# Two-layer hybrid trunk with a routed expert layer: the heads of the expert rounds split from the loop, a second feature buffer, and a PSUM bank of its own for the last down product

## The chip, the cores and the metric

The kernel runs on one core of a Trainium2 chip. The metric is the time of one execution on the device in microseconds (us); lower is better. The engines are TensorE (PE in the profile, its weight loads PEld), VectorE (DVE), ScalarE (ACT), GpSimd (POOL) and SyncE (SP). They run side by side and wait for each other through semaphores only.

## The reference, cut to what matters

Two layers run over 256 context tokens and 256 latent tokens of width 1024, all in float32. Each has a mixer (retention, state-space scan, neighbourhood attention), which the change leaves alone, and then a mixture of 16 experts of which every token takes two:

```python
def moe_ffn(h, router_w, router_b, w_gate, w_up, w_down):
    t = h.reshape(-1, shp[-1])
    aff = jax.nn.sigmoid((t @ router_w).astype(jnp.float32))
    ...  # best group of four experts, then its top 2: idx; gates = affinities over their sum
    # each chosen expert e:  (silu(t @ w_gate[e]) * (t @ w_up[e])) @ w_down[e]
    # weighted by the gate, summed over the two, times a gate row of the layer, added to the stream
```

Layer 0 routes 512 tokens (T = 4 tiles of 128), layer 1 only the 256 latent ones (T = 2). The expert weights of a layer are 16 x 3 x 2 MB, and all of them are read.

## The kernel before, in words

`route` (DVE) finds the chosen experts and gates. `assign` (DVE, L1980 to L2011) counts the tokens of each expert, ranks the experts by load, gives each a capacity (128, 96 or 64 slots by rank), works out how many rounds R are needed (an overfull expert needs a second one; here one runs), writes the order of the experts to `order_i`, from which SP reads which weights to load, and at its end (L2008 to L2011) works out `place`, each token's slot in its expert. Experts 0 and 1 always have the first two ranks, since `route` sets their keys so.

Then every engine loads the number of rounds into a register (`load_rounds`) and enters a loop over rounds. DVE opens it with the memset L2164, whose semaphore `round_dve` the other engines wait for. An expert position q goes through these steps. The positions are grouped in units of one gather: a big or middle expert is a unit of its own, two small ones share one.

- `slots_of(u)` (DVE, three operations, L2032, L2037, L2040): which token owns each slot of unit u, as a one-hot sum; `who(u)` on PE (L1153) turns it into a column, `who(u)` on DVE (L2047) makes the indices `slot_i`, and POOL gathers the rows of the tokens (`gather`, L2314).
- `turn_x(u)` (PE, L1162) transposes the rows and ACT copies them (L1512) to one half of `XT`.
- `wide(q, 0)` and `wide(q, 1)` (PE, L1185, L1188, L1191) are the gate and up products, ACT's `silu` (L1519) and DVE's `product` (L2055) make the feature `hp`, `turn_h(q)` (PE, L1201) transposes it, ACT's `turned_h` (L1528) copies it to `hT`, `down(q)` (PE, L1217, L1221) is the down product to bank 3 (with bank 4 where it is wide), and DVE's `result` (L2069, for the joined ones L2066) takes it to `Yb`.
- ACT stores `Yb` to DRAM (L1536, L1540). After the last expert, POOL gathers each token's two rows back (L2340), ACT scales one (L1568), and DVE adds, gates and adds to `h` (L2136 to L2141 in layer 1, L2156 to L2161 in layer 0).

The order on PE is written by hand: in position q come wide(q, 0), turn_h(q-1), wide(q, 1), then turn_x and who of later units, then down(q-1). SP's queue issues the loads of the weights in order over 8 buffers (L682), each when the product that read the buffer before is done; the first load past the six early ones also waits for both first gathers.

In layer 1 the last two positions are "joined": they are not stored and gathered back, but a product with a slot matrix (`join`, L1248) puts them onto the tokens, and DVE adds that to `h` (`add_joined`, L2148). There the last down product already has bank 4 for itself, there are two `hT` buffers, and turn_h(15) stands ahead of down(14). In layer 0 there is one `hT`, and turn_h(15) comes after down(14):

```python
                        if plan.joined and q == NE - 1:
                            turn_h(r, q)
                        if q > 0:
                            down(r, q - 1)
                    ...
                    if not plan.joined:
                        turn_h(r, NE - 1)
                    down(r, NE - 1)
```

At the end of layer 1, DVE's queue has `add_gathered(0)` ahead of `result(14)`, and `add_gathered(1)` ahead of `result(15)`; each is three operations over 128x1024.

## Time and profile before

| | us |
|---|---|
| median of 3 runs (lowest, highest) | 1318.07 (1317.95, 1320.23) |
| the profiled execution | 1317.74 |
| its span, first to last instruction | 1315.9 |
| TensorE busy, share of the span | 1161.7, 88% |
| mean granted TensorE clock | 0.947 |
| DMA | 318.87 MB, mean 242 GB/s |

The span is the part of the execution that the profile shows; 1.84 us of the profiled execution lie outside it. All times in rows count from the span's start. "Idle before" stands in brackets with what ended it; a granted clock of 1.00 is 2.4 GHz and 0.50 is 1.2 GHz.

### The profile page before, as it was taken

How to read it: one execution, taken by the hardware profiler on the slowest of the kernel's cores; microseconds unless marked ns; L12 is line 12 of the kernel's file. 1: busy time of each engine (PE TensorE's matmuls, PEld its weight loads, DVE VectorE, ACT ScalarE, POOL GpSimd, SP SyncE). 2: the span in 40 equal slices, each digit the busy share in tenths (PEclk: the TensorE clock that was granted, in tenths of full speed). 3: DMA queues.
4: the chain of work that ended last, by engine and by line, in shares of the span. 5: the costliest groups of instructions: out<-in, count | busy, mean ns of one | idle time of the engine just before them, and what ended most of it. 6: DMA issues, size and time to landing. Idle time of an engine off the chain costs nothing.

```text
span 1315.9 us, 17739 instructions
## 1 busy us (share of the span) xinstructions
PE 1161.7 (88%) x7360; PEld 653.9 (50%) x7360; DVE 403.9 (31%) x759; ACT 219.7 (17%) x417; POOL 136.1 (10%) x118
## 2 busy tenths in 40 slices
PE   4899998999999389999999189998999579999875
PEld 1444444767644245654564055554865355645442
DVE  0131123794322741212111423034832531111004
ACT  2120221112220411110010222131121210111101
POOL 0002011550000010000000200211400010000001
PEclk9799999989999779999999689999999879999998
DMA  9222114652370478999997541137517469999995
GB/s 380 108 109 78 65 64 172 245 191 80 134 299 9 184 281 339 399 425 422 427 424 268 165 169 64 64 128 261 218 65 320 160 268 374 411 426 426 428 427 216
DMA packets 34481, 318.87 MB, mean 242 GB/s; under 512 B 6497, under 2 KB 7649, under 8 KB 16737
## 3 DMA queue, kind: packets, MB, share of 16 engines
q1 hardware_dynamic: 22432, 292.03, 55.3%
q10 hardware_dynamic: 7072, 13.11, 2.8%
q0 software_dynamic: 4896, 12.59, 2.7%
q8 instruction: 59, 0.97, 0.3%
q14 instruction: 22, 0.17, 0.0%
HBM read 308.79 MB, written 14.16 MB: 245 GB/s over the span
## 4 chain that ended last, share of the span: by engine, by line
PE 77%; DMA 11%; DVE 7%; ACT 2%; issue 2%; SPq 0%; POOL 0%; DVEq 0%; ACTq 0%; POOLq 0%
PE ps L843 14%; PE ps L1185 12%; PE ps L1087 6%; PE ps L830 6%; PE ps L1217 6%; PE ps L1188 4%; DMA ring<-in_w_mod 3%; DMA arena<-in_w_down 3%; PE ps L776 3%; PE ps L1191 2%; PE ps L1000 2%; DMA arena<-in_w_gate 2%; PE ps L1226 2%; PE ps L1162 2%; PE ps L1016 2%
## 5 line engine op out<-in xcount | busy, mean ns | idle before, releaser
L843 PE MATMUL ps<-ring,featT 128*128 128x512 f32 (+1 forms) x480 | 186.9, 550 | 0.0
L843 PEld LDWEIGHTS ps<-ring,featT 128*128 128x128 f32 x480 | 90.7, 190 | 92.3 <-issue 89.9
L1185 PE MATMUL ps<-arena 128*64 128x256 f32 x896 | 104.5, 387 | 5.9 <-ACT arena L1512 2.4
L2055 DVE TENSOR_TENSOR arena<-arena,ps 128x256 f32<-128x256 f32 (+2 forms) x32 | 15.6, 488 | 254.5 <-PE ps L1185 132.1
L1185 PEld LDWEIGHTS ps<-arena 128*64 128x64 f32 x896 | 64.7, 139 | 43.4 <-issue 15.8
L830 PE MATMUL ps<-featT,ring 128*128 128x512 f32 (+1 forms) x192 | 82.5, 588 | 2.3 <-ACT featT L1337 2.3
L1087 PE MATMUL ps<-ring,featT 128*128 128x512 f32 x192 | 82.7, 592 | 0.0
L2069 DVE COPY arena<-ps 128x512 f32<-128x512 f32 (+2 forms) x30 | 25.0, 834 | 142.2 <-PE ps L1217 65.5
L2314 POOL DMA_INDIRECT arena<-ffn_rows,slot_i x22 | 24.1, 1094 | 412.0 <-DVE slot_i L2047 412.0
L1519 ACT ACTIVATE arena<-ps 128x256 f32<-128x256 f32 (+2 forms) x32 | 14.0, 437 | 308.6 <-PE ps L1185 144.4
L1188 PE MATMUL ps<-arena 128*128 128x512 f32 x128 | 59.5, 622 | 2.3 <-ACT arena L1512 2.3
L830 PEld LDWEIGHTS ps<-featT,ring 128*128 128x128 f32 x192 | 36.8, 194 | 45.8 <-issue 42.6
L1087 PEld LDWEIGHTS ps<-ring,featT 128*128 128x128 f32 x192 | 36.5, 190 | 45.9 <-issue 45.9
L806 PE MATMUL ps<-const,tokA 128*128 128x128 f32 x112 | 20.3, 360 | 37.7 <-DVE tokA L1639 35.9
L1217 PE MATMUL ps<-arena 128*64 128x512 f32 x192 | 47.6, 605 | 3.8 <-DMA arena<-in_w_down 3.8
L776 PE MATMUL ps<-ring,silT 128*32 128x256 f32 (+1 forms) x656 | 48.0, 413 | 0.0
L1185 PE MATMUL ps<-ring,arena 128*64 128x256 f32 x384 | 44.1, 382 | 3.7 <-DMA ring<-in_w_gate 2.6
L1512 ACT ACTIVATE arena<-ps 128x1024 f32<-128x1024 f32 x22 | 22.5, 1023 | 124.6 <-PE ps L1162 124.6
L1188 PEld LDWEIGHTS ps<-arena 128*128 128x128 f32 x128 | 24.9, 199 | 33.6 <-issue 32.1
L2233 POOL TENSOR_TENSOR stat<-stat,pw 128x5 f32<-128x5 f32 (+2 forms) x14 | 14.6, 1044 | 258.2 <-DVE stat L1634 213.2
L806 PEld LDWEIGHTS ps<-const,tokA 128*128 128x128 f32 x112 | 18.5, 191 | 42.3 <-DVE tokA L1639 38.4
L1672 DVE COPY arena<-ps 128x512 f32<-128x512 f32 (+1 forms) x16 | 10.0, 625 | 93.1 <-PE ps L843 93.1
(314 smaller groups left out, 1611.2 us busy)
## 6 DMA issues: line engine op xcount, KB each, us to landing
ring<-in_w_mod SPq DMA_DIRECT2D x21, 2048.0 KB, 8.2
arena<-in_w_up SPq DMA_DIRECT2D x20, 2048.0 KB, 16.7
arena<-in_w_gate SPq DMA_DIRECT2D x16, 2048.0 KB, 16.8
ring<-in_w_down SPq DMA_DIRECT2D x12, 2048.0 KB, 13.3
arena<-in_w_down SPq DMA_DIRECT2D x12, 2048.0 KB, 17.7
ring<-in_w_in SPq DMA_DIRECT2D x10, 2048.0 KB, 7.9
ring<-in_w_gate SPq DMA_DIRECT2D x8, 2048.0 KB, 18.9
ring<-in_w_out SPq DMA_DIRECT2D x4, 2048.0 KB, 8.3
```

The lines of the kernel that those rows point to most:

```text
L776: i = mm(mod_row(l, u)[g:g + 32, :], silT[:, k, :], piece(q)[:, k, c:c + mod_width(l)], start=k < 4, stop=k >= 4)
L806: i = tr(ps[:, 1 + k % 4, P * t:P * t + P], tokA[:, t, P * k:P * k + P], ident)
L830: o = mm(bank[:, lo:TOK], W[:, k, c:c + P], featT[:, k, lo:TOK], start=k == 0, stop=k == KD - 1)
L843: o = mm(bank[:, lo:hi], featT[:, k, P * i:P * i + P], W[:, k, lo:hi], start=k == 0, stop=k == KD - 1)
L1000: i = mm(ps[:, 6 + t // 2, 256 * (t % 2):256 * (t % 2) + 256], featT[:, k, P * t:P * t + P], nvw[:, k, :], start=k == 0, stop=k == KD - 1)
L1016: i = mm(ps[:, n % 2, 0:keys], naT[s, hd // 2, P * t:P * t + P], naT[s, 2 + hd // 2, 0:keys], start=True, stop=not lat)
L1087: i = mm(ps[:, 4 + n % 2, :], featT[:, k, P * t:P * t + P], piece(p)[:, k, :], start=k == 0, stop=k == KD - 1)
L1162: o = tr(ps[:, 5 + k // 4, P * (k % 4):P * (k % 4) + P], gathered[u % 2][:, P * k:P * k + P], ident)
L1185: o = mm(ps[64 * half:64 * half + 64, m, 0:256], X_[:, k, at:at + SMALL_CAP], W[:, k, 256 * half:256 * half + 256], start=k == 0, stop=k = ...
L1188: o = mm(ps[:, m, :], X_[:, k, :], W[:, k, :], start=k == 0, stop=k == KD - 1)
L1191: o = mm(ps[32 * g:32 * g + 32, m, 256:384], X_[:, k, SMALL_CAP:SMALL_CAP + 32], W[:, k, P * g:P * g + P], start=k == 0, stop=k == KD - 1)
L1217: o = mm(ps[64 * out_half:64 * out_half + 64, to, :], H_[:, b, 64 * half:64 * half + 64], W[:, k, 512 * out_half:512 * out_half + 512], st ...
```

## The change

It has four parts, besides the counts of the semaphores that follow from them.

1. **Heads.** `place` is worked out at the start of `assign`, and slots_of, who and gather of units 0 and 1 leave the loop: slots_of(0) follows `place`, the others are put between the steps that rank the experts. PE and POOL do their parts ahead of `load_rounds`. Inside the loop each round now prepares the first two units of the round after it, also in the last round, where no token is left for them: per layer two more slots_of, who and gather. For that the subtraction from `place` (L2197) moves from the round's end to the position that opens the last unit but one.
2. **Layer 0's last product.** `hT` has two buffers in layer 0 too, turn_h(15) comes ahead of down(14), and down(15) goes to bank 4 and waits for result(13) only. ACT's turned_h(15) goes ahead of store(14).
3. **Layer 1's results.** Every `result` multiplies by the layer's gate row, in two operations over 64 partitions (six for a middle expert). ACT's scaling and one DVE operation for each tile drop out: `add_gathered` becomes two operations straight onto `h`.
4. **Layer 1's end.** DVE's order is result(14), add_gathered(0), result(15), add_gathered(1), add_joined. The rows gathered back go to other buffers.

```diff
 PE
@@ experts @@
+                for u in range(2):
+                    who(round_of(l, rounds_run[-1], 0), u)
+                first, R = load_rounds(pe, l)
+                rounds_run.append(R)
                 with pe.Fori(0, R) as n_round:
                     pe.wait_ge(S("round_dve"), r.all + (l + 1))
-                    who(r, 0)
-                    who(r, 1)
                     turn_x(r, 0)
...
-                        if plan.opens(q) and u + 2 < len(units):
+                        if plan.opens(q):
+                            if plan.joined and u + 1 == len(units):
+                                pe.wait_ge(S("slots_act"), n_round + 1)
                             who(r, u + 2)
-                        if plan.joined and q == NE - 1:
+                        if q == NE - 1:
                             turn_h(r, q)
                         if q > 0:
                             down(r, q - 1)
-                    if not plan.joined:
-                        turn_h(r, NE - 1)
                     down(r, NE - 1)
@@ down @@
-                    last = q == NE - 1 and q in plan.joined
+                    last = q == NE - 1
                     if q > 0:
                         pe.wait_ge(S("y_dve"), r.all * NE + (q - 1 if last else q))
                     to = 4 if last else 3
-                    H_ = hT_joined[q % 2] if plan.joined else hT
+                    H_ = hT_two[q % 2]
 ACT
@@ experts @@
+                        if q == NE - 1:
+                            turned_h(r, q)
                         if q > 0 and q - 1 not in plan.joined:
                             store(r, q - 1)
...
-                    turned_h(r, NE - 1)
                     if not plan.joined:
                         store(r, NE - 1)
-                    for i in range(T):
+                    for i in range(0 if plan.joined else T):
 DVE
@@ assign @@
+                link(V.tensor_scalar(pl, heads(ps[:, 3, 0:NE * T], T), 4096.0, None, ALU.add))
+                link(V.tensor_tensor(pl[:, 1:T, :], pl[:, 1:T, :], sums[:, 0:T - 1, :], ALU.add))
+                link(V.tensor_tensor(pl, pl, ch, ALU.mult))
+                link(V.tensor_scalar(pl, pl, -4096.0, None, ALU.add))
+                r = round_of(l, rounds_run[-1], 0)
+                slots_of(l, r, 0)
                 link(V.scalar_tensor_tensor(key[:, 2:NE], count[:, 2:NE], float(NE), iota[:, 2:NE], ALU.mult, ALU.subtract))
                 link(V.tensor_tensor(perm[:, :, :], repeat(key, NE), spread(key, NE), ALU.is_gt))
+                who(l, r, 0)
+                slots_of(l, r, 1)
                 link(V.tensor_reduce(rank, perm[:, :, :], AX.X, ALU.add))
                 ...
+                who(l, r, 1)
                 link(V.reciprocal(load_of, capE))
                 ...
-                (the four lines of place)
@@ result, layer 1 @@
-                    if q in plan.joined:
+                    if plan.joined:
+                        bank = 4 if q == NE - 1 else 3
                         for half in range(2):
                             s = slice(64 * half, 64 * half + 64)
-                            o = V.tensor_tensor(Yb[s, q % 2, 0:512], ps[s, 3 + q % 2, :], grow[s, 1, 512 * half:512 * half + 512], ALU.mult)
+                            o = V.tensor_tensor(Yb[s, q % 2, 0:512], ps[s, bank, :], grow[s, 1, 512 * half:512 * half + 512], ALU.mult)
+                        for g in range(4 if plan.middle(q) else 0):
+                            s = slice(32 * g, 32 * g + 32)
+                            o = V.tensor_tensor(Yb[s, q % 2, 512:768], ps[s, 4, 0:256], grow[s, 1, 256 * g:256 * g + 256], ALU.mult)
@@ add_gathered @@
+                    for n in range(2):
+                        ...
+                        V.scalar_tensor_tensor(h[:, t, :], back_joined[q - 1 + n], gate2[:, 1 - n, t:t + 1], h[:, t, :], ALU.mult, ALU.add
+                                               ).then_inc(S(("both_dve", "gated_dve")[n]), 1)
@@ experts @@
-                    for u in range(2):
-                        slots_of(r, u)
-                        who(r, u)
                     rows_of_round(r)
                     for q in range(NE):
                         u = plan.unit_of(q)
-                        if plan.opens(q) and u + 2 < len(units):
-                            slots_of(r, u + 2)
+                        if plan.opens(q) and u + 2 == len(units):
+                            V.tensor_tensor(pl, pl, repeat(capE, T), ALU.subtract).then_inc(S("row_steps"), 1)
+                            ...
+                        if plan.opens(q):
+                            slots_of(l, r, u + 2)
                         product(r, q)
-                        if plan.opens(q) and u + 2 < len(units):
-                            who(r, u + 2)
-                        if plan.joined and q == NE - 1:
-                            add_gathered(0)
+                        if plan.opens(q):
+                            who(l, r, u + 2)
                         if q > 0:
                             result(r, q - 1)
                     if plan.joined:
-                        add_gathered(1)
+                        add_gathered(0)
                     result(r, NE - 1)
                     if plan.joined:
+                        add_gathered(1)
                         for i in range(T):
                             add_joined(i)
...
+                    for c in range(2):
+                        dve.wait_ge(S(f"gathered{c}"), r.gathers + (len(units) // 2 * 16 + 16))
 POOL
@@ experts @@
+                for u in range(2):
+                    gather(round_of(l, of_layer_0, 0), u)
+                first, R = load_rounds(pool, l)
                 with pool.Fori(0, R) as n_round:
                     pool.wait_ge(S("round_dve"), r.all + (l + 1))
-                    for u in range(len(units)):
+                    for u in range(2, len(units) + 2):
                         gather(r, u)
```

## Rows read from the trace of the kernel before

**Rows 1.** The page: POOL's DMA queue (packets, MB, share); the chain that ended last.

```profile
q0 software_dynamic: 4896, 12.59, 2.7%
...
PE 77%; DMA 11%; DVE 7%; ACT 2%; issue 2%; SPq 0%; POOL 0%; DVEq 0%; ACTq 0%; POOLq 0%
```

**Rows 2.** Stretches of layer 1: busy us (instructions) by engine, clock, DMA share, GB/s.

```profile
1060.00:1070.00 10.00, 8.04 (x60) 5.25 (x64) 5.33 (x23) 2.31 (x2) 0.93 (x1) 0.60 0.57 200
...
1116.00:1118.00 2.00, 2.00 (x19) 1.09 (x17) 0.00 (x0) 0.00 (x0) 0.00 (x0) 1.00 0.78 270
...
1260.00:1270.00 10.00, 7.72 (x58) 4.48 (x56) 0.69 (x1) 0.75 (x2) 0.00 (x0) 1.00 1.01 429
```

**Rows 3.** Timeline of layer 0's head: start, us, engine, line, operation, idle before.

```profile
448.40 0.17 DVE L1986 SCALAR_TENSOR_TENSOR arena<-arena,const 128x14 f32<-128x14 f32 x1
...
453.62 0.22 DVE L2008 TENSOR_SCALAR arena<-ps 128x64 f32<-128x64 f32 x1
...
455.56 0.06 DVE L2164 MEMSET arena<- 128x1 f32 x1 [0.98 <-DVE arena L2011]
...
455.80 0.69 DVE L2032 TENSOR_TENSOR arena<-const,arena 128x512 f32<-128x512 f32 x1 [0.19 <-issue]
...
458.33 0.59 PE L1153 MATMUL ps<-const,arena 128*128 128x1 f32 x2 [11.28 <-DVE arena L2040]
...
464.74 1.97 PE L1162 MATMUL ps<-const,arena 128*128 128x128 f32 x8 [2.61 <-DMA arena<-ffn_rows,slot_i]
```

**Rows 4.** Timeline of layer 1's head.

```profile
1054.20 0.06 DVE L2164 MEMSET arena<- 128x1 f32 x1 [1.34 <-issue]
...
1054.36 0.43 DVE L2032 TENSOR_TENSOR arena<-const,arena 128x256 f32<-128x256 f32 x1
...
1055.76 0.59 PE L1153 MATMUL ps<-const,arena 128*128 128x1 f32 x2 [9.20 <-DVE arena L2040]
...
1060.76 1.97 PE L1162 MATMUL ps<-const,arena 128*128 128x128 f32 x8 [2.33 <-DMA arena<-ffn_rows,slot_i]
```

**Rows 5.** Timeline of layer 0's end.

```profile
721.27 0.42 DVE L2055 TENSOR_TENSOR arena<-arena,ps 128x256 f32<-128x256 f32 x1 [6.66 <-PE ps L1185]
...
724.53 0.44 PE L1201 MATMUL ps<-const,arena 128*128 128x128 f32 x2
...
727.10 3.65 PE L1217 MATMUL ps<-ring,arena 128*64 128x512 f32 x16 [2.13 <-ACT arena L1528]
...
757.10 0.23 DVE L2197 TENSOR_TENSOR arena<-arena 128x64 f32<-128x64 f32 x1 [0.16 <-DVE h L2161]
```

**Rows 6.** Timeline of the SP queue in layer 1: weight loads.

```profile
1064.22 0.35 SPq L682 DMA_DIRECT2D featT<-in_w_gate  x1
...
1117.04 0.33 SPq L682 DMA_DIRECT2D arena<-in_w_up  x1
```

**Rows 7.** Chain in order of time, layer 1: start, us, what.

```profile
1181.80 3.43 PE ps L1217 x16
...
1193.80 3.58 PE ps L1217 x16
```

**Rows 8.** Timeline of layer 1's end.

```profile
1278.04 0.69 DVE L2069 COPY arena<-ps 128x512 f32<-128x512 f32 x1 [4.84 <-PE ps L1217]
...
1293.83 0.94 POOL L2340 DMA_INDIRECT h<-expert_rows,arena  x1 [0.31 <-issue]
...
1294.70 3.65 PE L1217 MATMUL ps<-ring,arena 128*64 128x512 f32 x16 [1.25 <-DMA ring<-in_w_down]
...
1297.28 1.28 DVE L2136 SCALAR_TENSOR_TENSOR arena<-h,arena 128x1024 f32<-128x1024 f32 x1 [8.62 <-DMA h<-expert_rows,arena]
...
1301.00 1.38 DVE L2066 TENSOR_TENSOR arena<-ps,arena 64x512 f32<-64x512 f32 x2
...
1306.25 1.39 DVE L2066 TENSOR_TENSOR arena<-ps,arena 64x512 f32<-64x512 f32 x2
...
1311.61 1.22 DVE L2148 TENSOR_TENSOR h<-h,ps 128x1024 f32<-128x1024 f32 x1 [0.48 <-PE ps L1248]
```

More of the change, by code:

```diff
@@ L564, in trunk @@
         PLANS = [Plan(*TIERS[l], ORDERS[l], (NE - 2, NE - 1) if l == DEPTH - 1 else ()) for l in range(DEPTH)]
+        assert all(p.small(NE - 1) for p in PLANS)
         for q in PLANS[DEPTH - 1].joined:
@@ L1968, in route, with slots_of, who @@
                 link(V.tensor_tensor(ga, ga, spread(rsum[:, t0:NT], NE), ALU.mult))
+            rounds_run = [0]
+            def slots_of(l, r, u):
+                T, t0 = len(tiles(l)), tiles(l)[0]
+                plan = PLANS[l]
+                units = plan.units()
+                if u >= 2 or l > 0:
+                    dve.wait_ge(S("who_pe"), r.heads + (u - 1))
+                if u >= 1 or l > 0:
+                    dve.wait_ge(S("onehot_dve"), r.heads + u)
+                qs = units[u % len(units)]
+                v = plan.ranks[qs[0]]
+                n, each = len(qs), P // len(qs)
+                src = placeR if 2 <= u < len(units) else place
+                hot = onehot[:, 0:T, :]
+                V.tensor_tensor(hot.rearrange("p t (a s) -> p t a s", a=n),
+                                const[:, C_IOTA:C_IOTA + each].unsqueeze(1).unsqueeze(1).to_broadcast([P, T, n, each]),
+                                src[:, t0:NT, v:v + n].unsqueeze(3).to_broadcast([P, T, n, each]), ALU.is_equal
+                                ).then_inc(S("hot_steps"), 1)
+                dve.wait_ge(S("hot_steps"), 2 * r.heads + (2 * u + 1))
+                V.tensor_tensor(hot, hot, spread(const[:, C_TOK:C_TOK + T], P), ALU.mult
+                                ).then_inc(S("hot_steps"), 1)
+                dve.wait_ge(S("hot_steps"), 2 * r.heads + (2 * u + 2))
+                V.tensor_reduce(owner[:, u % 2, :], hot.rearrange("p t s -> p s t"), AX.X, ALU.add
+                                ).then_inc(S("onehot_dve"), 1)
+            def who(l, r, u):
+                dve.wait_ge(S("who_pe"), r.heads + (u + 1))
+                if u >= 2:
+                    dve.wait_ge(S(f"gathered{u % 2}"), r.gathers + (u // 2) * 16)
+                V.tensor_scalar(slot_i[:, u % 2:u % 2 + 1], ps[:, 7, 0:1], NO_TOKEN, None, ALU.add).then_inc(S("who_dve"), 1)
             def assign(l):
@@ L2308, in gather @@
                 def gather(r, u):
-                    pool.wait_ge(S("who_dve"), r.units + (u + 1))
+                    pool.wait_ge(S("who_dve"), r.heads + (u + 1))
                     if u >= 2:
@@ L2326, in experts @@
                     if plan.joined:
[L2327 removed]
+                        pool.wait_ge(S("up_pe"), r.all * NE + (NE - 2))
                     else:
```

97 lines of the change are left out of this document (31 added, 66 removed).

## The prediction

> **What bounds the kernel now.** I read the page first: TensorE has 77% of the chain that ended last, DMA 11%, VectorE 7% [rows 1]. That is a mean over stages, so I then read the stretches of the two expert stages, and in each looked for what ends last.
>
> In layer 0 TensorE never waits for weights: it runs without a gap from the first product to the last, and the stage is as long as TensorE's work. Time can be won there only ahead of the first product, where TensorE stands idle through a chain of small VectorE operations (it sat 11.28 us before who(0), and 2.61 us more for the gather [rows 3]), and behind the last ones.
>
> Layer 1 begins so too: in 1116 to 1118 the DMA share is 0.78, since the load at 1117.04 had to wait for TensorE [rows 2, 6]. From there on it does not fall again; in 1260 to 1270 it is 1.01 at 429 GB/s and TensorE is busy for 7.72 of 10 us [rows 2]. So the second half is bound by the weight stream. But that stream's last gap is closed by a product of TensorE, so an earlier TensorE moves the whole stream. Behind it stands a tail of VectorE work: down(15) ends at 1294.70 + 3.65 = 1298.35, the last addition at 1312.83 [rows 8].
>
> **Heads.** Nothing of the VectorE chain is dropped ahead of the first product; its order changes. Today the memset that opens the round stands at 455.56, and behind it come slots_of(0), who(0), the gather and turn_x(0) at 464.74 [rows 3]. Afterwards two slots_of and two who stand ahead of the memset. A slots_of takes 458.33 - 455.80 = 2.53 us in layer 0 and 1055.76 - 1054.36 = 1.40 in layer 1 [rows 3, 4]; who on VectorE I take at 0.1, below the 0.22 of another small operation there [rows 3]. TensorE's part of who is covered by the ranking steps that stand between. Memset: 455.56 + 2 x 2.53 + 2 x 0.1 = 460.8; turn_x(0) some 0.15 behind it, 461.0.
>
> Is the gather there by then? slots_of(0) starts at 448.40 plus the four operations of `place`, at most 455.56 - 453.62 = 1.94 together with the register loads. The one-hot is ready at 452.9, and from one-hot to turn_x went 464.74 - 458.33 = 6.41 us [rows 3]: 459.3, 1.7 us before it is needed. So the round's opening releases turn_x(0), no longer the gather. Layer 0 gains 464.74 - 461.0 = **3.7 us**. In layer 1 the memset comes at 1054.20 + 2.8 + 0.2 = 1057.2, turn_x at 1057.35 instead of 1060.76: **3.4 us**; one-hot to turn_x took only 5.00 us there [rows 4], so the gather is early again. Bounds: 2 us in each if every new wait costs a few tenths; 5.4 if the gather alone set it (459.3).
>
> In layer 1 the first of the later weight loads, now at 1064.22 behind both gathers [rows 6], can start up to 5 us earlier. I count nothing for it beyond the 3.4: the loads behind it wait for TensorE, up to the one at 1117.04.
>
> **Extra units.** Each layer gets two more who on TensorE. Cold, the pair of passes took 0.59 [rows 3]; warm and in the stream I take 0.15 each, **+0.3 us** in layer 0 (bounds 0 and 1.2) and nothing in layer 1, where TensorE waits for weights by then. VectorE's slots_of, 2.53 us at most, and the moved subtraction lie beside the gate and up products. From one down product to the next went 1193.80 - 1181.80 = 12.0 us, of which the down product itself is 3.4, so VectorE has over 8 us between them [rows 7]. The four empty gathers stand on POOL's queue ahead of the gathers back, which wait for the stores anyway, so they hold up nothing there. They do put packets into the DMA queues. POOL's queue had 4896 packets for 34 indirect DMAs, 144 each; its 12.59 MB are 3072 rows of 4 KB, so 1824 packets carried no row [rows 1]. Its share, 2.7% of the span, is 35.5 us; 12.59 MB at 429 GB/s are 29.3 [rows 1, 2]; 6.2 us are left for the 1824, 0.5 for a gather of 144. Only layer 1's two lie in a bound stream: **+1.0 us** (bounds: nothing, and 2.4 if each moved 128 rows of 4 KB).
>
> A page gives another price for them: the Trainium skill, "DMA: Bandwidth & Descriptors", section "Measured (HBM→SBUF, 128 partitions, SWDGE, issued from GpSimd)", names a floor of about 10.5 ns per packet. As an estimate from that page, 144 packets would take 1.5 us and two such gathers 3.0, which would bring the sum 2.0 us higher than the rows do. What the trace shows, packets that cost about a third of that on average, is what I take.
>
> **Layer 0's last product.** Today hp(15) is ready at 721.27 + 0.42 = 721.69, but turn_h(15) waits behind down(14) until 724.53, then for ACT's copy, so that down(15) starts at 727.10 [rows 5]. Afterwards TensorE idles for hp from 721.2, does turn_h to 722.25 (0.44), then down(14) in the 3.35 us it took (721.2 to 724.53) to 725.6, and down(15) directly behind: its `hT` is ready under down(14), its bank is its own. Gain 727.10 - 725.6 = **1.5 us**. result(14) comes 1.1 us later, but the last store, which the gathers back wait for, hangs on down(15). Bounds 1.0 and 2.1.
>
> L2197 stood on the chain at the layer's boundary with 0.23 us; two waits long since met take its place: **0.2 us**.
>
> **Layer 1's results.** Each small result becomes two operations of 64 partitions, 1.38 us for the pair against 0.69 for the copy; a middle one gets six, which I put at 2.9 [rows 8]. This lies in the 8 us between down products [rows 7]; if that cover were gone, it would be the rival below. One place is open: result(13) releases the store that the gathers back wait for, so these come 0.7 us later.
>
> **Layer 1's end.** Today `add_gathered(0)` started when the second gather landed, 1297.28, and result(15) had to wait for both add_gathered, to 1306.25, 8 us after down(15) had ended [rows 8]. Afterwards (stream unshifted): the second gather at 1297.9, two operations of 1.28 with the first already begun, to 1299.2; result(15) to 1300.65; add_gathered(1) to 1303.25 (its last gather was issued at 1293.83, and landing like the second takes it to about 1300.5); join beside it, done at the latest 1311.61 - 1307.64 = 3.97 us after result(15), at 1304.6; the last add_joined, 1.22, to 1305.85. Against 1312.83 that is **7.0 us**. Bounds: 5, if late gathers or the join end last; 8, if result(15) starts as soon as down(15) ends.
>
> **Sum.** 3.7 + 1.5 + 0.2 - 0.3 = 5.1 in layer 0; 3.4 - 1.0 + 7.0 = 9.4 in layer 1; 14.5 together. The profiled execution took 1317.74, so 1303.2; the median of the runs is 0.33 higher: **1303.5 us**.
>
> **Rivals.**
> (a) The stream of layer 1 does not follow: if DMA were the bound from its first load on, only that load's time would count and TensorE's earlier start would be lost, 1303.5 + 3.4 = 1306.9. For it speaks the share of 1.01 at the end; against it the gap at 1116 to 1118 [rows 2].
> (b) The reordering of layer 1's end brings only its lower bound, since the gathers back, issued under full DMA load, come later than today: 1305.5. For it, 8.62 us of VectorE's waiting for just that gather [rows 8]; against it, that they ran after the stores at the same distance from the stream's end.
> (c) More than forecast: the heads reach the gather's time (1.7 more in layer 0 and as much in layer 1) and the empty gathers cost nothing: 1299.1. Against it stands the order of the chain, which no one shortened.
> (d) Layer 0's new order does not do what it is to do, since turn_h(15)'s stall ahead of down(14) eats the gain: 1305.0. Layer 1 runs this order already, but there weights end last, so its trace does not settle it.
> (e) Slower: the doubled results get onto TensorE's path in layer 1. If down(q+1) waited for result(q) at every position, it would be 12 x 1.38 + 4 x 2.9 = 28 us, 1331. It decides once VectorE's work between two down products (product, slots_of, two or six result operations, at most about 6 us) passes the 8 us [rows 7]. I see nothing that takes it there.
>
> TensorE's clock adds spread to all: in 1060 to 1070 it was granted 0.60 on the mean, so four fifths of that stretch ran at 1.2 GHz after the idle head [rows 2]. If the rise comes 2 us earlier or later against the work, that is 1 us each way in each layer.
>
> **How the numbers follow.** Forecast within 1301 to 1305.3: 0.57. (a) 0.13, (b) 0.09, (d) 0.06, (c) 0.10, (e) 0.02, no measurable change for reasons I don't see 0.03. The range reaches from (c)'s edge to a little beyond (a): 1299.5 to 1307.5. A change under 0.2% (2.6 us) can't be told from none here. Faster 0.94, same 0.03, slower 0.03.
>
> **What would show it.** Layer 0: turn_x(0) near 461, released by VectorE's memset and not by the gather; down(15) directly behind down(14), no transposition between; the last expert product some 5 us earlier. Layer 1: turn_x(0) about 3.4 us closer to the stage's start, the weight stream's end as far, result(15) within 1.5 us of down(15)'s end, and the last addition 7 to 8 us behind down(15) and not 14.5. POOL's queue: 38 indirect DMAs, 5472 packets, bytes unchanged. The forecast fails if the empty gathers move rows, if down products wait for VectorE, or if the stream's start, not TensorE, sets its end.

## The result

The changed kernel takes **1300.28 us** (median of 4 runs, 1299.15 to 1306.51) against 1319.15 for the kernel before on the same chip (4 runs, 1317.95 to 1321.6). The ratio is 0.9872, 95% interval 0.9844 to 0.9900. The profiled execution took 1300.2, its span is 1298.4, its mean granted clock 0.953. Forecast were 1303.5 with a range of 1299.5 to 1307.5. Two later timings of the same kernel (e1, e12) gave 1303.98 and 1303.20, each timed beside the kernel before, 16.2 and 14.8 us below it; the two medians here are 18.9 us apart. Three executions on record came out some 2% longer at a lower granted clock; in e3, e9 and e10, where they stand, the medians given are over the other runs.

The span fell by 1315.9 - 1298.4 = 17.5 us. To see where, I cut both traces at the same events and subtracted. Each line begins where the one above it ends; won and forecast are in us:

| from | to | before | after | won | forecast |
|---|---|---|---|---|---|
| start | first router operation of layer 0 on VectorE | 440.2 | 438.7 | 1.5 | 0 |
| there | turn_x(0), layer 0 | 24.51 | 20.18 | 4.3 | 3.7 |
| there | last expert product on VectorE, layer 0 | 256.53 | 255.88 | 0.65 | -0.3 |
| there | end of down(15), layer 0 | 9.48 | 7.93 | 1.55 | 1.5 |
| there | first router operation of layer 1 | 309.67 | 309.97 | -0.3 | 0.2 |
| there | turn_x(0), layer 1 | 20.34 | 17.07 | 3.3 | 3.4 |
| there | start of down(15), layer 1 | 233.94 | 234.34 | -0.4 | -1.0 |
| end of down(15) | end of the last addition | 14.48 | 7.42 | 7.1 | 7.0 |
| there | end of span | 3.07 | 3.27 | -0.2 | 0 |

The first line lies ahead of everything that the change touches. Over the fourteen profiles of this case (both kernels and twelve experiments) that point falls between 435.4 and 442.5 us, so the 1.5 us are chance: e1, the same kernel again, has 441.2. The other large ones are the change's, as the experiments show.

**The page of the changed kernel**, POOL's queue and the chain that ended last:

```profile
q0 software_dynamic: 5472, 12.59, 2.8%
...
PE 78%; DMA 11%; DVE 7%; ACT 2%; issue 2%; SPq 0%; POOL 0%; DVEq 0%; ACTq 0%; POOLq 0%
```

It has 576 packets more than before and the same bytes [rows 1]: four gathers of 144 packets in which no row moves. The shares of the chain hardly differ; what was won was won at the edges of stages.

**Layer 0's head**, timeline of the changed kernel:

```profile
447.84 0.69 DVE L1991 TENSOR_TENSOR arena<-const,arena 128x512 f32<-128x512 f32 x1
448.56 0.69 DVE L1996 TENSOR_TENSOR arena<-arena,const 128x512 f32<-128x512 f32 x1
449.29 1.02 DVE L1999 TENSOR_REDUCE arena<-arena 128x128 f32<-128x512 f32 x1
...
451.12 0.16 DVE L2007 TENSOR_SCALAR slot_i<-ps 128x1 uint32<-128x1 f32 x1 [0.28 <-PE ps L1157]
...
452.71 1.22 POOL L2332 DMA_INDIRECT arena<-ffn_rows,slot_i  x1 [24.71 <-issue]
...
455.67 0.99 POOL L2332 DMA_INDIRECT arena<-ffn_rows,slot_i  x1 [1.75 <-DVE slot_i L2007]
...
458.67 0.06 DVE L2182 MEMSET arena<- 128x1 f32 x1 [0.40 <-issue]
...
458.87 1.97 PE L1166 MATMUL ps<-const,arena 128*128 128x128 f32 x8 [4.58 <-DVE arena L2182]
```

Both gathers are issued before the memset that opens the round. TensorE's wait ahead of turn_x(0) is ended by VectorE's L2182, where before it was ended by the gather's DMA [rows 3]. VectorE's own wait ahead of the memset shrank from 0.98 to 0.40.

**Layer 1's head**, with the SP queue:

```profile
1049.44 0.06 DVE L2182 MEMSET arena<- 128x1 f32 x1 [1.00 <-issue]
...
1049.72 1.96 PE L1166 MATMUL ps<-const,arena 128*128 128x128 f32 x8 [5.19 <-DVE arena L2182]
...
1050.60 0.35 SPq L685 DMA_DIRECT2D featT<-in_w_gate  x1
...
1105.64 0.33 SPq L685 DMA_DIRECT2D arena<-in_w_up  x1
```

The first late load is issued 0.88 us after turn_x(0) starts, before it was 3.46 [rows 4, 6]. The load that waited for TensorE at 1117.04 comes 55.92 us after turn_x(0), before it was 56.28: it follows TensorE, not its own queue.

**Layer 0's end** answers to [rows 5]:

```profile
714.75 0.42 DVE L2072 TENSOR_TENSOR arena<-arena,ps 128x256 f32<-128x256 f32 x1 [6.66 <-PE ps L1189]
715.23 0.44 PE L1205 MATMUL ps<-const,arena 128*128 128x128 f32 x2 [0.58 <-DVE arena L2072]
715.59 3.65 PE L1221 MATMUL ps<-tokA,arena 128*64 128x512 f32 x16
...
719.08 3.60 PE L1221 MATMUL ps<-ring,arena 128*64 128x512 f32 x16
719.38 0.69 DVE L2090 COPY arena<-ps 128x512 f32<-128x512 f32 x1 [4.21 <-PE ps L1221]
```

down(15) starts at 719.08, while result(14) only begins to empty the shared bank at 719.38. A wait of 0.58 took the place of one of 2.13 [rows 5].

**Layer 1's end** answers to [rows 8]:

```profile
1280.88 0.96 POOL L2361 DMA_INDIRECT arena<-expert_rows,arena  x1 [16.99 <-DMA expert_rows<-arena]
...
1284.06 3.65 PE L1221 MATMUL ps<-ring,arena 128*64 128x512 f32 x16 [1.75 <-DMA ring<-in_w_down]
...
1285.25 1.28 DVE L2158 SCALAR_TENSOR_TENSOR h<-arena,h 128x1024 f32<-128x1024 f32 x1 [1.42 <-DMA arena<-expert_rows,arena]
...
1287.40 1.29 DVE L2158 SCALAR_TENSOR_TENSOR h<-h,arena 128x1024 f32<-128x1024 f32 x1 [0.86 <-DMA h<-expert_rows,arena]
...
1288.72 1.39 DVE L2084 TENSOR_TENSOR arena<-ps,arena 64x512 f32<-64x512 f32 x2
...
1292.78 2.35 DVE L2166 TENSOR_TENSOR h<-h,ps 128x1024 f32<-128x1024 f32 x2
```

down(15) ends at 1284.06 + 3.65 = 1287.71 and result(15) starts 1.0 us later, not 7.9. It still waits a little: add_gathered(0) stood idle for the second gather back (0.86).

### The profile page after: what moved, and what is told of

It reads as the page before. It is cut to its first block, busy times and chain, and to the rows that moved or that the text cites. A ratio compares the mean times of both kernels' runs of the same rounds, so it can differ in the third digit from the quotient of the medians.

```text
span 1298.4 us, 17851 instructions
## 1 busy us (share of the span) xinstructions
PE 1156.4 (89%) x7368; PEld 652.2 (50%) x7368; DVE 425.1 (33%) x803; ACT 217.5 (17%) x415; POOL 138.4 (11%) x122
## 4 chain that ended last, share of the span: by engine, by line
PE 78%; DMA 11%; DVE 7%; ACT 2%; issue 2%; SPq 0%; POOL 0%; DVEq 0%; ACTq 0%; POOLq 0%
PE ps L846 14%; PE ps L1189 13%; PE ps L1090 6%; PE ps L833 6%; PE ps L1221 6%; PE ps L1192 4%; DMA ring<-in_w_mod 3%; DMA arena<-in_w_down 3%; PE ps L779 3%; PE ps L1195 2%; PE ps L1003 2%; DMA arena<-in_w_gate 2%; PE ps L1230 2%; PE ps L1166 2%; PE ps L1019 2%
## 5 line engine op out<-in xcount | busy, mean ns | idle before, releaser
L2084 DVE TENSOR_TENSOR arena<-ps,arena 64x512 f32<-64x512 f32 x32 | 22.0, 689 | 67.4 <-PE ps L1221 42.5
L2090 DVE COPY arena<-ps 128x512 f32<-128x512 f32 (+2 forms) x16 | 14.3, 892 | 78.0 <-PE ps L1230 27.2
## 6 DMA issues: line engine op xcount, KB each, us to landing
arena<-in_w_down SPq DMA_DIRECT2D x12, 2048.0 KB, 17.5
ring<-in_w_gate SPq DMA_DIRECT2D x8, 2048.0 KB, 17.5
```

## The experiments

The experiments come in three groups, each timed on one chip together with the kernel before: e1 to e4 (kernel before 1320.13), e5 to e8 (1320.46), e9 to e12 (1317.98). The changed kernel's median moved by up to 3.7 us from one group to the next, and an interval reaches some 3 us to each side, so the distance between events inside the profiles carries the verdicts where a term is smaller than that.

**e1: the changed kernel again.** No edit.

> The changed kernel once more, beside the others of this call. Of the 17.5 us by which its profiled span was shorter than that of the kernel before, 1.5 were there before the changed code begins (the router product of layer 0 at 434.6 instead of 436.1). My theory: that is spread in TensorE's clock during the opening, no work of the change. Then this run's span splits again into 4.3 (head of layer 0), 1.5 (its end), 3.3 (head of layer 1) and 7.1 (its end), while the opening comes out anywhere within 2 us. Rival: the change moves the opening too, and the router product stands at 434.6 again in every run of it. Time: 1300 to 1303.

Measured 1303.98 us (1300.15 to 1305.43, 6 runs), ratio 0.9870 (0.9848 to 0.9892). Router operation at 441.2; heads (from the router's first VectorE operation to turn_x(0)) 20.11 and 17.08 us; layer 0's last product 7.93; the last addition ends 8.14 us behind down(15). So 3.7 us of the median are spread from one group to the next. The heads and layer 0's last product repeat within 0.1 us, both expert stages and layer 1's end only within 0.7.

**e2: the heads back in the loop**, and with them no unit prepared in vain.

```diff
-                for u in range(2):
-                    who(round_of(l, rounds_run[-1], 0), u)
...
-                r = round_of(l, rounds_run[-1], 0)
-                slots_of(l, r, 0)
-                who(l, r, 0)
...
+                    for u in range(2):
+                        slots_of(l, r, u)
+                        who(l, r, u)
                     rows_of_round(r)
...
-                    for u in range(2, len(units) + 2):
+                    for u in range(len(units)):
                         gather(r, u)
```

> The changed kernel with its first part undone: place is worked out at the end of the ranking, slots_of, who and gather of units 0 and 1 stand inside the loop behind the round's opening, and no units of a next round are prepared (right for a single round only, which is what these inputs need). My theory: turn_x(0) falls back to about 24.5 us behind the router's first VectorE operation in layer 0 and about 20.3 in layer 1, 4.3 and 3.3 us later than with the change, and layer 1's weight stream with it: 7.0 to 7.6 us slower than the changed kernel, 1307 to 1309. Rival: layer 1's stream does not follow the head, so only layer 0's share is lost, 4.3 us, 1305.

Measured 1309.09 us (1307.53 to 1312.87), ratio 0.9916 (0.9896 to 0.9936). TensorE's wait ahead of turn_x(0) is ended by the gather again, in both layers:

```profile
467.07 1.97 PE L1166 MATMUL ps<-const,arena 128*128 128x128 f32 x8 [2.72 <-DMA arena<-ffn_rows,slot_i]
...
1062.33 1.97 PE L1166 MATMUL ps<-const,arena 128*128 128x128 f32 x8 [2.93 <-DMA arena<-ffn_rows,slot_i]
```

The heads take 24.56 and 21.21 us, against 20.21 and 16.91 in e3, which differs from e2 in nothing else: 4.3 us in each layer, 8.6 together. The medians are 9.0 us apart, so layer 1's weight stream gave nothing of the gain back that these runs could show. Two things in e2's profile do not fit this neatly. Its head in layer 1 is 0.9 us longer than that of the kernel before (20.34), whose order it restores; 0.6 of it lies between the gather's issue and turn_x(0) (3.95 against 3.35 us). So the change itself won 3.3 us there and not 4.3. And from turn_x(0) to down(15) it took 235.27 us, 1.5 more than e3. The cause of either is open.

**e3: heads split, but without the extra units.** The counts of the semaphores follow.

```diff
-                        if plan.opens(q):
+                        if plan.opens(q) and u + 2 < len(units):
                             slots_of(l, r, u + 2)
...
-                    for u in range(2, len(units) + 2):
+                    for u in range(2, len(units)):
                         gather(r, u)
```

It prepares nothing for a round that follows, so it only serves inputs that need one round, as these do.

> The changed kernel without the two units that each round prepares for the next one (two slots_of, who and gather per layer; right for a single round only). The heads stay as changed. My theory, by the trace of the kernel before: 0.3 us on TensorE in layer 0 and 1.0 us in layer 1's weight stream come back, 1.3 us together, of which the stream's part is read as the time from the load that closes the last gap to the start of down(15). Rival, by the floor per packet that a page of the Trainium skill states: 3.0 us in the stream. Second rival: nothing at all, since packets without rows take no time that a transfer would use. POOL's queue goes back to 4896 packets.

Measured 1300.10 us (five runs, 1295.78 to 1302.10), ratio 0.9836 (0.9811 to 0.9861), against 1303.98 for e1 on the same chip; the intervals overlap by a hair. In layer 1's stream nothing gets shorter: 177.78 us from the load that TensorE releases to down(15), against 177.71 in e1 and 177.66 before. Layer 0's stage took 255.25 us, 1.3 less than in e1, but only 0.2 below the shortest trace with the extra units. What clearly gets shorter is the end:

```profile
1270.58 1.10 ACTq L1539 DMA_DIRECT2D expert_rows<-arena  x2
...
1281.65 0.96 POOL L2357 DMA_INDIRECT arena<-expert_rows,arena  x1 [71.52 <-DMA expert_rows<-arena]
...
1286.79 1.28 DVE L2156 SCALAR_TENSOR_TENSOR h<-arena,h 128x1024 f32<-128x1024 f32 x1 [0.83 <-DMA arena<-expert_rows,arena]
1288.26 1.28 DVE L2156 SCALAR_TENSOR_TENSOR h<-h,arena 128x1024 f32<-128x1024 f32 x1 [0.18 <-DMA h<-expert_rows,arena]
1289.58 1.39 DVE L2082 TENSOR_TENSOR arena<-ps,arena 64x512 f32<-64x512 f32 x2
```

From the issue of the store of result(13) to the first gather back went 1281.65 - 1270.58 = 11.07 us. In e1 it went from 1272.23 to 1284.73, 12.50. VectorE is therefore done with add_gathered(0) just as down(15) ends (1289.46), and the last addition ends 6.52 us behind it instead of 8.14.

**e4: the round opened earlier.** The memset that opens the round, and its wait, moved ahead of the ranking steps that the loop's first operations don't need.

```diff
+                dve.wait_ge(S("row1"), upto("row1", l, len(segs(l))))
+                V.memset(few[:, 0:1], 0.0).then_inc(S("round_dve"), 1)
                 ...
-                dve.wait_ge(S("row1"), upto("row1", l, len(segs(l))))
-                V.memset(few[:, 0:1], 0.0).then_inc(S("round_dve"), 1)
```

> The changed kernel with the memset that opens the round moved ahead of the operations that write the order of the experts, right behind the number of rounds. My theory: in the changed kernel turn_x(0) is released by the round's opening and no longer by the gather. So now it is released by the gather or the register loads of TensorE: 1.4 to 1.6 us earlier in layer 0 (near 18.7 us behind the router's first VectorE operation instead of 20.2) and 1.5 to 1.8 earlier in layer 1, and as much off the total, 3.2 us, 1297.5. Rival: the gather is what ends last all the same, and nothing moves. Second rival: the gain of layer 1 is lost in the weight stream, since the load behind both gathers does not come earlier: 1.5 us only.

Measured 1301.59 us (1297.28 to 1302.3), ratio 0.9852 (0.9829 to 0.9875), 2.4 below e1 with overlapping intervals. The heads are 18.78 and 15.92 us: 1.3 and 1.2 shorter than in e1. In layer 0 this is as far as it goes:

```profile
457.83 0.06 DVE L2049 MEMSET arena<- 128x1 f32 x1
459.07 0.29 PEld L1166 LDWEIGHTS ps<-const,arena 128*128 128x128 f32 x2 [3.32 <-DMA arena<-ffn_rows,slot_i]
459.08 0.47 PE L1166 MATMUL ps<-const,arena 128*128 128x128 f32 x1 [3.24 <-DMA arena<-ffn_rows,slot_i]
```

turn_x(0) starts 1.25 us behind the memset, and its releaser is the gather again. In the changed kernel the opening is what ends last; 1.4 us below it lies the gather. In layer 1 the profile shows no releaser ahead of turn_x(0) any more (4.02 us, "issue"), so what stops it there is open; from turn_x(0) to down(15) went 234.13 us, so the earlier start was kept.

**e5: the kernel before with one thing changed**, the order at layer 1's end.

```diff
-                        if plan.joined and q == NE - 1:
-                            add_gathered(0)
...
                     if plan.joined:
-                        add_gathered(1)
+                        add_gathered(0)
                     result(r, NE - 1)
                     if plan.joined:
+                        add_gathered(1)
```

> The kernel before, with VectorE's order at layer 1's end alone changed: result(14), add_gathered(0), result(15), add_gathered(1), add_joined, each add_gathered still three operations and ScalarE still scaling. It tells what of the 7.1 us at layer 1's end the order gave and what the shorter additions. My theory: the order alone gives 4 us. The second gather sets the start, three operations of 1.25 take 3.75, result(15) ends 5.1 us after that start instead of 10.3, and behind it stand three operations and two additions, so the last addition ends 11.4 us after the second gather's landing instead of 15.5. The rest, 3 us, is the work that the gate in the results removed. Time 1314. Rival: the order gives all of it, since result(15) then comes at once behind down(15): 1311. Second rival: nothing, since VectorE is bound by its own work there: 1318.

Measured 1314.77 us (1312.1 to 1319.58, 12 runs), ratio 0.9964 (0.9948 to 0.9981). The last addition ends 10.36 us behind down(15), before 14.48. Of the 7.1 us at layer 1's end the order alone brings 14.48 - 10.36 = 4.1. The rest, 2.9, is what `add_gathered` no longer does, less what the extra units cost there: against e3, which has none either, the distance falls from 10.36 to 6.52, so the shorter additions are worth 3.8, and the extra units take 0.9 back (7.42). Here each row of `add_gathered` still takes three operations,

```profile
1298.45 1.28 DVE L2136 SCALAR_TENSOR_TENSOR arena<-h,arena 128x1024 f32<-128x1024 f32 x1 [2.31 <-DMA h<-expert_rows,arena]
1299.77 1.23 DVE L2139 TENSOR_TENSOR arena<-arena 128x1024 f32<-128x1024 f32 x1
1301.02 1.23 DVE L2141 TENSOR_TENSOR h<-h,arena 128x1024 f32<-128x1024 f32 x1
1302.28 1.39 DVE L2066 TENSOR_TENSOR arena<-ps,arena 64x512 f32<-64x512 f32 x2
```

**e6: the first late load held back** until TensorE's first turned rows have been copied.

```diff
+                sp.wait_ge(S("xT_act"), first * len(PLANS[0].units()) + 1)
```

> The changed kernel, with the first weight load behind the gathers made to wait for the first XT copy as well, about 2.2 us later against TensorE than in the changed kernel and about where it stood against TensorE before. My theory: in layer 1 the stream's last gap is closed by TensorE, so this costs nothing: from turn_x(0) to the start of down(15) 234.3 us as in the changed kernel, within 0.4. Rival: the stream is bound from its first load on, and the time from turn_x(0) to down(15) grows by the 2.2 us.

Measured 1300.88 us (1299.1 to 1304.7), ratio 0.9862 (0.9830 to 0.9894).

```profile
1052.13 0.35 SPq L685 DMA_DIRECT2D featT<-in_w_gate  x1
```

The load is issued 3.21 us after turn_x(0) (1048.92) instead of 0.88, nearly the distance it had before. From turn_x(0) to down(15) went 233.96 us, as in the others (233.3 to 234.4, e2 alone 235.3).

**e7: VectorE given more to do in layer 1.** Nine small results are each followed by a second pair of operations into a part of the buffer that nobody reads.

```diff
+                        if plan.small(q) and q < NE - 3:
+                            for half in range(2):
+                                s = slice(64 * half, 64 * half + 64)
+                                o = V.tensor_tensor(Yb[s, q % 2, 512:1024], ps[s, bank, :], grow[s, 1, 512 * half:512 * half + 512], ALU.mult)
```

> The changed kernel, where each small result of layer 1 up to position 12 is worked out twice, the second time into columns of Yb that nothing reads: nine more pairs, 12.5 us more work for VectorE. My theory: VectorE has over 8 us of cover between two down products, so the total stays within 0.5 us. Rival: result is on TensorE's path in layer 1, and the total grows by 1.4 us at each of them, 12.5 us, 1313.

Measured 1302.87 us (1298.46 to 1305.14), ratio 0.9862 (0.9828 to 0.9895). The 18 operations cost VectorE 12.4 us, and the stretch from turn_x(0) to down(15) stays at 233.80:

```profile
L2091 DVE TENSOR_TENSOR arena<-ps,arena 64x512 f32<-64x512 f32 x18 | 12.4, 688 | 0.2
```

**e8: layer 0's last product as before**, with one feature buffer and the shared bank; the rest of the change stays.

```diff
-                    last = q == NE - 1
+                    last = q == NE - 1 and q in plan.joined
-                    H_ = hT_two[q % 2]
+                    H_ = hT_two[q % 2] if plan.joined else hT
-                        if q == NE - 1:
+                        if plan.joined and q == NE - 1:
                             turn_h(r, q)
...
+                    if not plan.joined:
+                        turn_h(r, NE - 1)
                     down(r, NE - 1)
```

> The changed kernel with its second part undone: in layer 0 one hT, turn_h(15) behind down(14), the last down product in bank 3 behind result(14). My theory: from the last product of VectorE (hp of position 15) to the end of down(15) 9.5 us as in the kernel before instead of 8.0, and 1.5 us more in the total, 1302. Rival: the stall of TensorE for hp ahead of down(14) eats the gain, and the total does not move.

Measured 1306.45 us (1305.06 to 1307.58), ratio 0.9895 (0.9868 to 0.9921). The last product took 11.18 us, not 9.48. The timeline shows the old idle time of 2.13, and behind it a down(15) of 5.35 us instead of 3.65:

```profile
720.92 0.44 PE L1205 MATMUL ps<-const,arena 128*128 128x128 f32 x2
723.49 5.35 PE L1221 MATMUL ps<-ring,arena 128*64 128x512 f32 x16 [2.13 <-ACT arena L1536]
```

The windows of this stretch (length, busy time by engine, granted clock, DMA share, GB/s) say why:

```profile
721.00:723.00 2.00, 0.36 (x2) 0.12 (x2) 0.69 (x1) 0.00 (x0) 0.00 (x0) 1.00 0.43 173
723.00:725.00 2.00, 1.51 (x8) 0.57 (x10) 0.00 (x0) 0.38 (x1) 0.00 (x0) 0.93 0.56 124
725.00:727.00 2.00, 2.00 (x8) 0.65 (x6) 0.00 (x0) 0.00 (x0) 0.00 (x0) 0.50 0.00 0
727.00:729.00 2.00, 1.84 (x6) 0.24 (x2) 0.11 (x1) 0.00 (x0) 0.00 (x0) 0.71 0.00 0
```

Behind the pause of 2.13 us the clock stood at 0.50, the 1.2 GHz level, in 725 to 727. In the kernel before the same pause left it at 1.00, as its windows show, and so it did in e5, where down(15) took 3.65 us:

```profile
723.00:725.00 2.00, 1.97 (x10) 0.49 (x6) 0.27 (x1) 0.00 (x0) 0.00 (x0) 1.00 0.95 400
725.00:727.00 2.00, 0.00 (x0) 0.00 (x0) 0.43 (x1) 0.34 (x1) 0.00 (x0) 1.00 0.40 124
727.00:729.00 2.00, 1.90 (x10) 0.76 (x12) 0.00 (x0) 0.04 (x1) 0.00 (x0) 1.00 0.38 85
```

So part 2 is worth 9.48 - 7.93 = 1.55 us when the clock holds, and 11.18 - 7.93 = 3.25 when it falls. The median lies 5.6 and 3.6 us above e6 and e7, the changed kernel with small additions on the same chip; the intervals overlap.

**e9: layer 1's empty gathers behind the gathers back.** e3 left open whether the end is late through the two gathers or through the units' other work.

```diff
-                    for u in range(2, len(units) + 2):
+                    for u in range(2, len(units) + (0 if plan.joined else 2)):
                         gather(r, u)
...
                                              ).then_inc(S(f"back{q % 4}"), 16)
+                    if plan.joined:
+                        for u in range(len(units), len(units) + 2):
+                            gather(r, u)
```

POOL also waits for their landing at the round's end.

> The changed kernel, but in layer 1 the two gathers without rows are issued behind the last gather back instead of ahead of the first. Theory 1 (these two gathers hold up what comes on the same path late in layer 1): from the issue of the store of result 13 to the first gather back 11.1 us instead of 12.5, from the end of down(15) to the end of the last sum 6.5 us instead of 7.4 to 8.3, the total 1.1 us below the changed kernel of the same call; the stretch from the first turn of x in layer 1 to down(15) stays at 233.6 to 234.3. Rival (the extra lists of slots on DVE, ACT and TensorE cost it, not the gathers): 12.5 and 7.4 to 8.3 stay, the total stays. Second rival (the gathers only move their cost behind the sums): end as late as before by the wait for their landing, 7.4 or more, with the gathers back early.

Measured 1304.50 us (5 runs), ratio 0.9903 (0.9880 to 0.9926), against 1303.20 for e12. The gathers moved, the end did not:

```profile
1270.43 1.10 ACTq L1541 DMA_DIRECT2D expert_rows<-arena  x2
1282.42 0.96 POOL L2361 DMA_INDIRECT arena<-expert_rows,arena  x1 [72.51 <-DMA expert_rows<-arena]
...
1287.42 1.39 POOL L2332 DMA_INDIRECT arena<-ffn_rows,slot_i  x1 [0.30 <-issue]
...
1289.03 1.34 DVE L2158 SCALAR_TENSOR_TENSOR h<-h,arena 128x1024 f32<-128x1024 f32 x1 [1.10 <-DMA h<-expert_rows,arena]
```

From store to first gather back 11.99 us, from down(15) to the last addition 7.86. The gathers back are not as early as the 11.1 that theory 1 asks for, so theory 1 falls, and with it the second rival. What stands is the rival: something else about the extra units.

**e10: e4 and e9 together**, to see whether a version beats both kernels.

> The changed kernel with the opening of the round on DVE ahead of the placing work (turn of x 1.3 us earlier in each layer) and the gathers without rows of layer 1 behind the gathers back (1.1 us). If both add up: 3.7 us below the changed kernel of the same call, some 1297 if that is at 1301. Heads 18.8 and 15.9 us from the router to the first turn of x, end 6.5 us behind down(15). Rival (only the heads count): 2.6 below. Rival (loads set the stream of layer 1, so its earlier start is lost): 1.1 plus 1.4 of layer 0, 2.5 below, with 235.4 us from the first turn of x to down(15) in layer 1 instead of 234.

Measured 1302.04 us (5 runs), ratio 0.9875 (0.9853 to 0.9898), against 1303.20 for e12 (ratio 0.9886, 0.9864 to 0.9909). The heads are 18.79 and 15.94 us as in e4, so 2.8 us shorter than in e12; from store to first gather back went 12.30 us, and the end is 7.71 us behind down(15), so the late gathers brought nothing here either. Layer 1's stage took 234.37 us, e12's 234.27, so its earlier start was kept. Of 2.8 us the median shows 1.2, and the intervals overlap: not shown to be faster than the changed kernel.

**e11: layer 0's down(15) back in the shared bank**, the order and the two buffers kept.

```diff
-                    last = q == NE - 1
+                    last = q == NE - 1 and q in plan.joined
...
-                    V.tensor_copy(Yb[:, q % 2, 0:n], flat(4 if q == NE - 1 else 3, n)).then_inc(S("y_dve"), 1)
+                    V.tensor_copy(Yb[:, q % 2, 0:n], flat(3, n)).then_inc(S("y_dve"), 1)
```

> The changed kernel, but the closing down product of layer 0 shares its bank with the ones before it again, so that it waits until the result of expert 14 has been taken from the bank; the order of the turns and the two feature buffers stay. Theory 1 (the turn ahead and the bank each have their part): down(15) of layer 0 ends 8.7 us behind the start of the last up product instead of 7.93, total 0.8 us more than the changed kernel of the same call. Rival (result 14 is done before the turn anyway, the bank gives nothing): 7.93 and no difference. Second rival (the new idle time of TensorE lets the clock fall, as with the old order): 9.5 to 11.2.

Measured 1305.21 us (1302.84 to 1308.34), ratio 0.9906 (0.9884 to 0.9927), 2.0 above e12 with overlapping intervals.

```profile
715.71 3.65 PE L1221 MATMUL ps<-tokA,arena 128*64 128x512 f32 x16
...
719.50 0.69 DVE L2090 COPY arena<-ps 128x512 f32<-128x512 f32 x1 [4.21 <-PE ps L1221]
720.29 3.65 PE L1221 MATMUL ps<-ring,arena 128*64 128x512 f32 x16 [0.93 <-issue]
```

down(15) starts 0.10 us after result(14) has left the bank, at 9.08 us instead of 7.93. So turn and buffer alone bring 0.4 of part 2's 1.55 us, and the bank on top of them 1.15; the bank without them was not run. Without its own bank, down(15) trades most of the wait for the turned features (2.13 us) for one on result(14) (0.93). The clock held: the product took 3.65 us, so the second rival falls.

**e12: the changed kernel, third timing.** No edit.

> The changed kernel itself, timed beside the other three of this call: 1299 to 1304 by both its earlier medians; 7.4 to 8.3 us from the end of down(15) to the end of the last sum in layer 1, 12.5 us from the issue of the store of result 13 to the first gather back, 7.93 us in layer 0 from the start of the last up product to the end of down(15).

Measured 1303.20 us (1299.86 to 1306.61, 6 runs), ratio 0.9886 (0.9864 to 0.9909). Heads 20.49 and 17.08, last product 7.93, store to gather back 12.31, end 8.01.

## Why the prediction was right

**The total.** 14.5 us were forecast; the profiled pair shows 17.5, of which 1.5 lie ahead of the change. 14.5 of 1318.07 is a ratio of 0.989, inside the intervals of all three timings (0.9872, 0.9870, 0.9886). Part of this closeness is luck: the 1.0 us that I charged to the empty gathers in the stream was not there, and a cost of about that size, which I had not named, stood at the end.

**Heads, 3.7 and 3.4.** Measured 4.3 and 3.3, again in e1 (4.4 and 3.3). e2 against e3 gives 4.3 in each, in layer 1 more than the change won, for the reason given under e2. The releaser is the one forecast, the opening memset. What was a little off in layer 0 is the memset's own wait: I kept its 0.98 us, and it became 0.40. I had 1.7 us between the gather's landing and its use; e4 took 1.3 away in layer 0 and met the gather, so rival (c)'s first half was a real next step there, somewhat smaller than its 1.7, which this change does not take; in layer 1 the step was 1.2.

**The stream follows TensorE.** This carried 3.4 us against rival (a), and e6 and e2 settle it: issuing the first late load 2.3 us earlier is worth nothing, an earlier TensorE all of it. From turn_x(0) to down(15) the stage takes the same time wherever turn_x(0) stands: 233.9 us with the old head (before, e5), 233.6 to 234.3 in the three traces of the changed kernel. The row that told it ahead of time was the gap at 1116 to 1118 [rows 2]; the load that closes it comes 55.9 to 57.3 us behind turn_x(0) in every trace.

**Extra units, 0.3 in layer 0.** Below what can be seen. From turn_x(0) to the last product the ten traces with the extra units (after, e1, e4, e6 to e12) have 255.48 to 257.02 us, mean 256.17; the four without (before, e2, e3, e5) 255.25 to 256.53, mean 255.69. The difference of the means, 0.5, is smaller than either spread. The stage is also not quite "without a gap": in the kernel before one wait of 1.18 us for ACT's copy (L1512) lies in it, ahead of a product at 487.07.

**Empty gathers, 1.0 in layer 1's stream.** This term was wrong: no such cost shows in the stream. From the load that TensorE releases to down(15) went 177.54 to 178.42 us in the eight traces with them (mean 177.74; the highest is the changed kernel's first profile) and 177.41 to 178.00 in the six without (before, e2, e3, e5, e9, e10; mean 177.63): the means differ by 0.1. I divided a queue's time by its packets and took all of it as the stream's loss. In the changed kernel they are issued at 1233.13 and 1262.91, into a stream whose DMA share was 1.02 (1226 to 1236 and 1256 to 1266). The estimate from the floor per packet in the Trainium skill, "DMA: Bandwidth & Descriptors", section "Measured (HBM→SBUF, 128 partitions, SWDGE, issued from GpSimd)", 3.0 us, agrees with the traces even less. That floor is measured there on transfers that carry data; no run here measured such packets apart.

**A cost that I had not named** stands at layer 1's end instead. With the extra units the first gather back is issued 11.9 to 12.5 us after the store of result(13) (ten traces: after, e1, e4, e6 to e12), without them 11.07 to 11.31 (before, e2, e3, e5), and the last addition ends 7.4 to 8.3 us behind down(15) instead of 6.5 (e2, e3). That is 0.9 to 1.7 us, about my term of 1.0, at another place. e9 and e10 (11.99 and 12.30, without the two gathers ahead of it) show that neither these gathers' place in POOL's queue nor their packets are the cause. Nor is a shift of the weight loads: the last one ahead of the store is issued 11.8 us before it in e3 as in e1, and 11.1 before it in e10 as in e2. What the cause is stays open; the units' lists on VectorE, ScalarE and TensorE were not told apart.

**Layer 0's last product, 1.5.** Measured 1.55. Rival (d) falls: turn_h(15)'s stall is 0.58 us. By e8 the gain can be twice as much, through the clock, and by e11 three quarters of the 1.55 hang on the bank.

**L2197, 0.2.** Not seen: VectorE's idle time at the boundary grew by as much. From the last addition of layer 0 to the first operation of layer 1 went 757.54 - 756.94 = 0.60 us before and 749.58 - 748.96 = 0.62 after.

**Layer 1's results.** Hidden, as forecast; e7 adds 12.4 us more to VectorE without any effect on the stage (233.80). So rival (e) has at least another 1.4 us of room at each of nine positions; where it would begin was not looked for.

**Layer 1's end, 7.0.** Measured 7.1 in the profiled pair, 6.3 in e1, 6.5 in e12; 4.1 of it is the order (e5). The predicted order of events held, and my estimate of where VectorE would wait (the second gather back) too. Rival (b)'s lower bound of 5 was not reached; its mechanism, gathers back that come later, is the 0.9 to 1.7 us above.

## What to carry to other kernels

When a stage is bound by a stream of loads, find the load that waits for compute: if there is one, time saved ahead of compute's first operation can be worth its full length at the stream's end, as the 3.3 us were here, and issuing the first loads 2.3 us earlier was worth nothing. Read a head by what ends the wait of its first product, cut that, and stop at the next releaser, which the timeline already shows. Price a tail by what stands in line on its engine behind the last product; and where two products share a bank, look whether the second needs one of its own: the new order without it brought 0.4 of 1.55 us.

## What the runs showed of the hardware

- The same pause of TensorE, 2.13 us between a short transposition and the next product, left the granted clock at 1.00 in two traces (before, e5), and in a third (e8) the clock stood at 0.50 behind it, for some 3 us; the product behind it took 3.65 us in the two and 5.35 in the third. What decides is not settled by three traces.
- An indirect gather whose rows are all out of bounds still puts 144 packets on POOL's queue and takes POOL 0.99 us to issue in the changed kernel's trace, but moves no bytes, and two of them cost a saturated weight stream nothing that shows (mean 177.74 us with, 177.63 without).
- The distance from the issue of a store (here of result(13), in two DMAs of 128 KB) under a full stream to the issue of the gather that waits for its landing is not steady from kernel to kernel: 11.07 to 12.51 us, always under 11.4 in the four traces without the extra units and never under 11.9 in the ten with them.
